# The second block's mixer: attention beside the projection, mLSTM alone behind it

## The reference, cut to what matters

```python
def hybrid_mixer(h, w_in, gate_bias, g_q, g_k, g_mh, w_out):
    proj = h @ w_in          # mq mk mv mo mg aq ak av: 256 256 512 512 16 512 512 512
    gates = ... + gate_bias
    hm = bidirectional_mlstm(mq, mk / 8, mv, gates[0], log_sigmoid(gates[1]), gates[2], log_sigmoid(gates[3]))
    hm = rms_norm(hm, g_mh) * sigmoid(mo)                  # 4 heads, 128 wide
    qa = partial_rope(rms_norm(aq, g_q)) * 64 ** -0.5      # 8 heads, 64 wide
    ka = partial_rope(rms_norm(ak, g_k))
    ha = dilated_attention(qa, ka, av)                     # windows at dilations 1, 4, 16
    return concatenate([hm, ha]) @ w_out
```

## Time and profile before

| what | us |
|---|---|
| median of three runs | 3205.44 |
| the profiled execution | 3206.36 |
| its span, first to last instruction | 3204.4 |
| PE busy in the span | 3104.4 (97%) |
| DVE busy | 1905.7 (59%) |
| ACT busy | 1042.2 (33%) |
| mean granted clock of PE, as a share | 0.985 |
| projection of this mixer (2465.17 to 2631.09) | 165.92 |
| mixed stage (2631.09 to 2783.29) | 152.20 |
| output projection (from 2783.29 to 2835) | 51.71 |

### The profile page before, as it was taken

The page is one execution under the profiler, slowest core; times in us unless marked ns, Lnnn a source line. Parts: engine busy times, 40 slices in busy tenths (PEclk is TensorE's granted clock), DMA queues, the critical chain, the costliest instruction groups (busy, mean ns, idle before and its releaser), DMA issues.

```text
span 3204.4 us, 37150 instructions
## 1 busy us (share of the span) xinstructions
PE 3104.4 (97%) x15012; PEld 2517.3 (79%) x15022; DVE 1905.7 (59%) x2786; ACT 1042.2 (33%) x1525; POOL 9.7 (0%) x23
## 2 busy tenths in 40 slices
PE   8999999998899999999999999999999998899998
PEld 7888888786678888788877888878887765578887
DVE  7876654636665555666657555466665565564434
ACT  4212222435442222422235222332223435442222
POOL 0000000000000000000000000000000000000000
PEclk9999999999999999999999999999999998899999
DMA  6433342210033443256532353235451220133231
GB/s 228 144 119 119 137 146 79 65 52 11 2 125 132 143 173 124 82 178 233 187 117 71 131 186 130 87 115 190 169 215 57 79 66 1 47 121 103 92 99 53
DMA packets 102964, 369.19 MB, mean 115 GB/s; under 512 B 11358, under 2 KB 12638, under 8 KB 102540
## 3 DMA queue, kind: packets, MB, share of 16 engines
q1 hardware_dynamic: 101788, 362.14, 33.2%
q0 software_dynamic: 1008, 4.69, 0.4%
HBM read 364.69 MB, written 2.10 MB: 114 GB/s over the span
## 4 chain that ended last, share of the span: by engine, by line
PE 86%; DVE 8%; ACT 4%; issue 1%; DMA 1%; SPq 0%; POOL 0%; DVEq 0%; ACTq 0%; POOLq 0%
PE ps L193 25%; PE ps L195 24%; PE ps L194 24%; PE ps L197 4%; PE ps L198 2%; DVE SQ L615 1%; DVE HL L604 1%; DVE WL L185 1%; PE ps L2869 1%; DVE XT L1038 1%; DVE RAW L1501 0%; DVE DUMP L306 0%; ACT WH L180 0%; DMA STG<-in_w_modt 0%; PE ps L500 0%
## 5 line engine op out<-in xcount | busy, mean ns | idle before, releaser
L193 PE MATMUL ps<-HH,WH 128*128 128x512 f32 x2400 | 947.2, 395 | 5.4 <-ACT S L915 2.2
L195 PE MATMUL ps<-HH,WL 128*128 128x512 f32 x2400 | 936.4, 390 | 0.0
L194 PE MATMUL ps<-HL,WH 128*128 128x512 f32 x2400 | 936.0, 390 | 0.0
L180 ACT ACTIVATE WH<-RAW 128x1024 fp32r<-128x1024 f32 x456 | 459.0, 1048 | 630.9 <-PE ps L195 361.8
L185 DVE TENSOR_TENSOR WL<-RAW,WH 128x1024 fp32r<-128x1024 f32 x456 | 542.7, 1219 | 75.3 <-ACT WH L180 75.1
L193 PEld LDWEIGHTS ps<-HH,WH 128*128 128x128 f32 x2400 | 450.9, 188 | 111.3 <-issue 10.2
L195 PEld LDWEIGHTS ps<-HH,WL 128*128 128x128 f32 x2400 | 450.9, 188 | 96.8
L194 PEld LDWEIGHTS ps<-HL,WH 128*128 128x128 f32 x2400 | 451.2, 188 | 95.7 <-issue 3.8
L1038 DVE SCALAR_TENSOR_TENSOR XT<-ps,DER,XT 128x512 f32<-128x512 f32 x512 | 346.6, 683 | 246.5 <-PE ps L195 231.7
L193 PE MATMUL ps<-GH,WH 128*128 128x512 f32 x1056 | 414.1, 392 | 4.8 <-DVE GL L946 4.8
L195 PE MATMUL ps<-GH,WL 128*128 128x512 f32 x1056 | 411.1, 389 | 0.0
(11 more groups left out here) (373 smaller groups left out, 2600.0 us busy)
## 6 DMA issues: line engine op xcount, KB each, us to landing
RAW<-in_w_modt SPq DMA_DIRECT2D x200, 512.0 KB, 5.0
RAW<-in_ffn_wi SPq DMA_DIRECT2D x182, 512.0 KB, 4.9
RAW<-in_w_gu SPq DMA_DIRECT2D x90, 512.0 KB, 4.5
RAW<-in_ffn_wo SPq DMA_DIRECT2D x88, 512.0 KB, 4.7
RAW<-in_w_in SPq DMA_DIRECT2D x44, 512.0 KB, 3.6
RAW<-in_w_down SPq DMA_DIRECT2D x44, 512.0 KB, 3.9
RAW<-in_w_out SPq DMA_DIRECT2D x16, 512.0 KB, 4.4
STG<-in_w_modt SPq DMA_DIRECT2D x10, 512.0 KB, 12.9
```

The costliest lines, as they stand in the source:

```text
L180: act.e.activation(u.hi, u.ld.view, ACT.Copy).then_inc(u.hi_done.sem, 1)
L193: pe.e.matmul(out, wh, x[0], start=first, stop=False)
L194: pe.e.matmul(out, wh, x[1], start=False, stop=False)
L195: m = pe.e.matmul(out, wl, x[0], start=False, stop=last)
```

## The change

Attention's steps are put between the halves of the projection's chunks; mLSTM runs behind the projection with nothing beside it.

- `projection` gets `between`, called in the middle of every single chunk and behind its eviction. It draws the next step of `dilated`, which waits with empty steps until its pair's query and key are split.
- The projection has banks 0 and 1, all side work bank 2. `DilTrans` uses banks 6 and 3 from the start. `PP` and `PT` lie in the lent rooms.
- The chunks have another order: DQ, DK, DV and an mLSTM value chunk in turn, then MV3, the four MO, and MQ and MK last.
- `NormedRope` has four parts. Square root and reciprocal become Ln and Exp(-0.5 x) on ACT and three DVE operations (a Newton step); the scaling is a part of its own. One Ln-Exp table is loaded ahead of the projection. The sigmoid of MO moves out of the eviction to `MlSigmoid` behind the projection, and the Ln-Exp table is loaded again behind it.
- `MlExp` is split in `MlWeights` (ACT) and `MlScore` (PE), with weights one round ahead, six places for them instead of four, two score banks (0 and 1) instead of one, and two sets of summing banks by head (2, 3, 4 and 6, 7, 5). The eight broadcasts move from the projection into `mlstm`: two ahead of it and two in each of heads 0 to 2.
- `MixSplit` of attention's four row blocks comes in the rounds of head 1. The last head's quotient, square, root and turn follow the last sum with nothing between.

```diff
 class NormedRope(Step):
...
-            act.e.activation(ti.RS, P.banks[self.b], ACT.Sqrt, scale=1.0 / 64, bias=P.EPSC).then_inc(st["root"].sem, 1)
+            act.e.activation(ti.RS, P.banks[self.b], ACT.Ln, scale=1.0 / 64, bias=P.EPSC).then_inc(self.ln.sem, 1)
+            act.wait_ge(*self.ln)
+            act.e.activation(ti.RS, ti.RS, ACT.Exp, scale=-0.5).then_inc(st["root"].sem, 1)
...
-            dve.e.reciprocal(ti.RS, ti.RS).then_inc(st["inv"].sem, 1)
+            dve.e.scalar_tensor_tensor(v, P.banks[self.b], EPS * 64, r, ALU.add, ALU.mult).then_inc(self.prod.sem, 1)
+            dve.wait_ge(*self.prod)
+            dve.e.scalar_tensor_tensor(v, v, -0.5 / 64, r, ALU.mult, ALU.mult).then_inc(self.half.sem, 1)
+            dve.wait_ge(*self.half)
+            dve.e.scalar_tensor_tensor(r, v, 1.5, r, ALU.add, ALU.mult).then_inc(st["inv"].sem, 1)
...
+class MlSigmoid(Step):
...
+        for h in range(4):
+            act.e.activation(m.O[:, h, :], m.O[:, h, :], ACT.Sigmoid).then_inc(m.opened[h].sem, 1)
...
+    def main(self, h):
+        return 2 if h % 2 == 0 else 6
+
+    def extra(self, h):
+        return 4 if h % 2 == 0 else 5
...
     def projection(self, pr, w, chunks, segs_of, evac, lag, beside=None, depth=1, between=None):
...
+                    if len(chs) == 1 and between:
+                        self.add(ProjMM(pr, [p], range(4)))
+                        between()
+                        self.add(ProjMM(pr, [p], range(4, 8)))
...
                     evac(p)
+                    if len(chs) == 1 and between:
+                        between()
...
-                pr = Proj(self, h, (0, 1, 2, 3), (4, 5, 6, 7))
+                pr = Proj(self, h, (0, 1), (2,))
...
-                order = [DQ, DV, MG, DV + 1, DQ + 1, DV + 2, DV + 3, DQ + 2, MQ, MQ + 1, DQ + 3, MK, MK + 1]
+                order = []
                 for i in range(4):
-                    order += [DK + i, MV + i]
-                order += list(range(MO, MG))
-                self.projection(pr, a["w_in_2"], order, lambda ch: [(0, T)], evac, lag)
...
+                    order += [DQ + i, DK + i, DV + i, MG if i == 0 else MV + i - 1]
+                order += [MV + 3] + list(range(MO, MG)) + [MQ, MK, MQ + 1, MK + 1]
+                self.projection(pr, a["w_in_2"], order, lambda ch: [(0, T)], evac, lag, between=lambda: next(steps, None))
+                for _ in steps:
+                    pass
+                self.add(MlSigmoid(m))
+                self.add(LogExpTable())
...
     def mlstm(self, m, w, mix, w_out):
...
+        for d in range(2):
+            self.add(MlBroadcast(m, 0, d))
+        self.add(MlMask(m, 0))
+        split(0, True)
+        split(0, False)
+        unit[0] = self.add(MlWeights(m, 0, 0))
         self.add(MlFloor(m))
...
+        self.add(MlTurnFloor(m, w.score[15].exp + [w.quot[3].done]))
+        for r in range(16):
+            h, j = r // 4, r % 4
+            self.add(MlScore(m, unit[r]))
+            if h and j == 1:
+                quot[h - 1] = self.add(MlQuot(m, den[h - 1]))
+            if r < 15:
+                unit[r + 1] = self.add(MlWeights(m, (r + 1) // 4, (r + 1) % 4))
+            if h and j == 1:
+                square[h - 1] = self.add(MlSquare(m, quot[h - 1]))
+            if r:
+                last[r - 1] = self.add(MlSum(m, unit[r - 1]))
+            self.add(MlProd(m, unit[r]))
+            if h and j == 0:
+                den[h - 1] = self.add(MlDen(m, last[r - 1]))
+            if h and j == 2:
+                root[h - 1] = self.add(MlRoot(m, square[h - 1]))
+            if h and j == 3:
+                out[h - 1] = self.add(MlOut(m, root[h - 1]))
+            if j == 2 and h < 3:
+                for d in range(2):
+                    self.add(MlBroadcast(m, h + 1, d))
+                self.add(MlMask(m, h + 1))
+            if h == 0 and j in (0, 1):
+                split(1, j == 0)
             if h == 1:
...
+                mixed(4 + j, w.quot[j].done)
+        last[15] = self.add(MlSum(m, unit[15]))
+        den[3] = self.add(MlDen(m, last[15]))
         self.new_ring()
         self.units = self.split([w_out[0]])
...
+        quot[3] = self.add(MlQuot(m, den[3]))
+        for k in range(2):
+            mixed(k, out[k].done)
+        square[3] = self.add(MlSquare(m, quot[3]))
+        root[3] = self.add(MlRoot(m, square[3]))
+        mixed(2, out[2].done)
+        out[3] = self.add(MlOut(m, root[3]))
+        mixed(3, out[3].done)
...
     def dilated(self, w):
...
+                while w.pairs[q][0] not in w.qsplit or w.pairs[q][0] not in w.ksplit:
+                    yield
                 self.add(DilScore(w, q))
-                yield
             if 1 <= q <= last:
                 self.add(DilTrans(w, 2 * q - 2))
-                yield
+            yield
+            if 1 <= q <= last:
...
                 self.add(DilTrans(w, 2 * q - 1))
...
                 self.add(DilPV(w, q - 2))
...
+            if q < last:
+                self.add(DilCount(w, q))
+            yield
```

More of the change, by code:

```diff
@@ L2177, in __init__ @@
             self.rsfree = tiles.rsfree
-            st["sum"] = tiles.sqfree = s["side_mm"].next()
-            st["root"] = pr.sidefree[self.b] = s["nr_act"].next()
-            st["inv"] = s["rope"].next()
+            st["sum"] = s["side_mm"].next()
+            self.ln, st["root"] = s["nr_act"].next(), s["nr_act"].next()
+            self.prod, self.half = s["rope"].next(), s["rope"].next()
+            st["inv"] = tiles.sqfree = s["rope"].next()
+            pr.sidefree[self.b] = self.prod
+        elif part == 2:
             st["scaled"] = tiles.rsfree = s["rope"].next()
@@ L2435, with __init__ @@
 class MlBroadcast(Step):
[L2438 to L2443, removed]
+    def __init__(self, m, h, d):
+        self.m, self.h, self.d, self.b = m, h, d, m.main(h) + d
+        self.split, self.free = m.mgsplit, m.numfree[h % 2]
+        self.spread = m.P.s["ml_mm"].next()
+        self.done = m.P.s["ml_act"].next()
         m.bcast[h, d] = self.done
+        if d == 1:
+            m.numfree[h % 2] = self.done
     def tensor(self, pe):
@@ L2455, in scalar, with __init__ @@
     def scalar(self, act):
+        m, h = self.m, self.h
+        act.wait_ge(*self.spread)
+        act.e.activation(m.MB[self.d * 4 + self.h], m.P.banks[self.b], ACT.Copy).then_inc(self.done.sem, 1)
+class MlSigmoid(Step):
+    def __init__(self, m):
+        self.m = m
+        m.opened = [m.P.s["ml_gate"].next() for _ in range(4)]
+    def scalar(self, act):
         m = self.m
[L2457 to L2460, removed]
+        for h in range(4):
+            act.e.activation(m.O[:, h, :], m.O[:, h, :], ACT.Sigmoid).then_inc(m.opened[h].sem, 1)
 class MlMask(Step):
@@ L2489, in __init__ @@
         for d in range(2):
-            s = m.na % 4
+            s = m.na % 6
             m.na += 1
@@ L2796, in scalar @@
                 act.wait_ge(*w.trans[u - 4].turned)
-            act.e.activation(w.PP[:, u % 4, :], w.P.banks[4 + par], ACT.Exp,
+            else:
+                for t in w.freed:
+                    act.wait_ge(*t)
+            act.e.activation(w.PP[u % 4], w.P.banks[4 + par], ACT.Exp,
                              bias=w.NM[:, s, hs:hs + 1]).then_inc(self.exp[par].sem, 1)
@@ L2845, in scalar @@
         act.wait_ge(*self.free)
-        act.e.activation(w.PT[:, self.u // 2 % 2, self.u % 2, :], w.P.banks[self.b], ACT.Copy).then_inc(self.done.sem, 1)
+        act.e.activation(w.PT[self.u % 4], w.P.banks[self.b], ACT.Copy).then_inc(self.done.sem, 1)
 class DilPV(Step):
@@ L2854, in __init__ @@
         self.j, self.n = w.pairs[q]
-        self.ready = [w.trans[2 * q + par].done for par in range(2)]
+        self.ready = [w.trans[2 * q + par].done for par in range(2)] + [w.turned[self.j]]
         self.done = w.P.s["dil_mm"].next()
@@ L3024, in at, with rooms @@
         return self.nc.alloc_sbuf_tensor_at(self.name(name), shape, dt, offset=address)
+    def rooms(self, places):
+        return [self.over_ring(f"ROOM{i}{part}", [128, 2, T], F32, part + i * 4096)[:, half, :]
+                for i in places for part in (0, NUNIT * 4096) for half in range(2)]
     def name(self, s):
@@ L3306, in follow, with projection @@
         lag.append(g)
-    def projection(self, pr, w, chunks, segs_of, evac, lag, beside=None, depth=1):
+    def projection(self, pr, w, chunks, segs_of, evac, lag, beside=None, depth=1, between=None):
         def job(chs):
@@ new lines, in split @@
+        def split(p, query):
+            x, hi, lo, splits = (m.Q, m.QH, m.QL, m.qsplit) if query else (m.K, m.KH, m.KL, m.ksplit)
+            splits[p] = self.add(HiLo(self, x[:, p, :], hi[:, p, :], lo[:, p, :], []))
+        mixed = lambda k, ready: self.add(MixSplit(self, mix, [k], [ready]))
+        unit, last, den, quot, square, root, out = {}, {}, {}, {}, {}, {}, {}
+        m.numfree[1] = m.turnfree[1] = w.quot[3].done
+        for d in range(2):
+            self.add(MlBroadcast(m, 0, d))
```

200 lines of the change are left out of this document (82 added, 118 removed).

## The result

The changed kernel took 3210.89 us (median of 20 runs, 3206.06 to 3219.80), the kernel before beside it 3205.38 (20 runs, 3200.77 to 3209.18): ratio 1.0020, 95% interval [1.0014, 1.0027]. I had forecast 3202.5, so the sign is wrong and the size is off by 8.4 us. The run that was profiled is the slowest of the 20 (3219.80), so what its trace shows of the clock is a bad case.

The account below looks back on a forecast made before the run. PE, busy 97% of the span, was taken as the bound. Projection +71.8, mixed stage -75.4 and output projection +0.7 gave -2.9 us: 3203.5 against the profiled 3206.36, median 3202.5, range 3188 to 3219.

Parts of the forecast that it names:

- The turns' waits: Projection: in seven chunks the turn behind a rotation waits 0.95 us for DVE's sine product to free the bank.
- the start: Start of mLSTM: a serial ACT chain behind the last projection product, 10.1 us with almost nothing for PE.
- the length of a stall: mLSTM rounds: PE waits 2.15 us for a DVE product in a head's second tile, three times.
- the tail: Behind the last mLSTM sum: the last head's quotient chain leaves PE idle 6.9 us before the last turn.
- the price of attention's PE work: Projection: attention's scores, transpositions, PV steps and spreads add 65.7 us of PE time at full clock.
- one side bank instead of four: Projection: bank waits of 8.3 us, from seven turns, 0.6 for the turn of U and 1 for late counts.
- Rival C: Projection: in-order queues make attention steps wait 2 us at each of eight norm parts, +13, 3219 us; chance 0.09.
- the output projection: Output projection: low clock at its beginning costs 2.5 us, early weight fetch removes the 1.8 us wait; +0.7.
- The clock of the rounds: mLSTM rounds: low clock for 12 us behind the start, +4.8, and 1.5 after each of three stalls, +4.5.
- Rival B: mLSTM rounds: mLSTM alone never earns full clock, stage 90 us, +11.5, 3217; sign granted clock below 0.6; chance 0.18.
- rival A: mLSTM rounds and after: the clock recovers fast and returns 12.2 us, -15, 3190 us; chance 0.24.
- D: End of projection: attention isn't done by the last chunk and runs on alone; three steps to spare; chance 0.02.

Follow-up runs that it names:

- a4: Changed kernel with the gate chunk moved from fourth place to behind the last value chunk: 3207.72 us, ratio 1.0000.
- b2: Changed kernel with two side banks (2 and 3) and one transposing bank (6) in place of one and two: 3202.42 us, ratio 0.9990.
- d4: Changed kernel with the next block's bias sum on DVE in two halves, one output chunk apart: 3206.24 us, ratio 1.0003.
- d1: Changed kernel with late gate chunk, sigmoids and table loads inside the projection, and two extra 128-row products per mLSTM score: 3194.72 us, ratio 0.9970.
- d2: Changed kernel with late gate chunk and sigmoids and table loads inside the projection, without extra products: 3204.15 us, ratio 0.9995.
- a1: Changed kernel with 15 filler products on PE in the pause before the first mLSTM score: 3210.7 us, ratio 1.0008.
- a2: Changed kernel with two extra 128-row products ahead of each mLSTM score: 3205.38 us, ratio 1.0002.
- a3: Changed kernel with both the filled start pause and two extra 128-row products a round: 3208.02 us, ratio 1.0007.

## Why the prediction was wrong

**What held.** The turns' waits (6.1 against 6.7), the hidden work of ACT and DVE in most of the projection, the start (9.7 against 10.1), no pause behind table loads, the length of a stall (1.9 against 2.15), the tail (6.6 against 6.9). a4, in which only the order of the gate chunk differs, has the projection that I forecast to 1 us, but two errors cancel in that: of its 236.92 us PE is busy 225.55, where I had priced 229.4 without waits, and idle 11.4, where I had 8.3. So the price of attention's PE work was right only to about 4 us.

**What failed, in order of size.**

1. In the step "one side bank instead of four", the 0.6 us for the turn of U. It measured 5.64, with low clock behind it: the projection took 243.1 against 237.7, +5.4. I had priced the bank as if the copy came when its producer ended, and didn't write down what stands ahead of it in DVE's queue: two scans, a norm part that they push back, ACT behind that, a weight's split behind ACT. That this queue is the cause, and not the bank's number by itself, is shown by a4 (another place for the gate chunk, and the wait is gone) and b2 (two side banks, and a pause of 5.66 at the same place). Rival C named this mechanism, in the wrong place: not 2 us at each of eight norm parts but 5 us where the gate chunk falls between two of them.
2. In the step "the output projection", the 1.8 us that should go. I took the wait for one on late weights. It was not: ACT had their high half ready at 2815.52, and DVE began the low half only at 2817.48, behind a bias sum, which d4 moves out of the way. The same sum stands in front of the same low half in the trace of the kernel before:

```profile
2802.28 3.61 DVE L752 SCALAR_TENSOR_TENSOR ACC<-RAW,MOD,ACC 128x256 f32<-128x256 f32 x7
...
2802.80 1.04 ACT L180 ACTIVATE WH<-RAW 128x1024 fp32r<-128x1024 f32 x1
...
2805.81 1.22 DVE L185 TENSOR_TENSOR WL<-RAW,WH 128x1024 fp32r<-128x1024 f32 x1
```

3. The clock of the rounds. I took 12 us of low clock behind the start and 1.5 for each stall. It is not a fixed price but varies from run to run: 0.50 through most of the rounds in the profiled run, and 72.6 to 84.8 us in the four traces of the same rounds. Rival B named the place and, for the profiled run (90 forecast, 84.8 measured), about the size; by the sign that I had set for it, a granted clock below 0.6, that run is B's (0.59 over the stretch). That the term was near the middle of the four is luck.

3202.5 + 5.4 + 1.8 = 3209.7, against 3210.9 measured. That the clock's term is right at the median is this sum's word and that of four traces, no more; the median run itself has no trace. From the other side: a4 took 3.2 off the median and d4 4.7. If the two add, which no run shows by itself, they leave 3203.0, near the 3202.5 that I had forecast.

Two slips of the working stand beside this. The range's low end, 3188, is said to be rival A with no stalls in the projection; by the terms above that is 3190 less 8.3, 3182. And the chance of "slower", 0.27, is less than the 0.29 of rivals B, C and D together.

Above the terms stands a wrong reading of the case: I counted the clock as a consequence of pauses alone. d1 and d2 have the same wait ahead of the rounds (3.8 us), and only d1 has the clock back. What PE ran in between decided there. Pauses still count: in a1's trace the clock falls behind a stall. The Trainium skill, "TensorE: Matmul & The Clock Gate", section "A second HAM failure mode: psum-queue depth-cycling", which I had put beside rival B, lays such a swinging clock to small pauses between groups of products; here it stays at 0.50 through 30 us without one pause, so pauses are not all of it. The Trainium skill, "ScalarE: Activation LUTs", section "What ACT_TABLE_LOAD costs", gives a drain of 1380 ns for every switch of the table set; that would be an estimated 2.8 us at the start, which the 0.02 us behind each load above exclude. Why two extra products hold the clock and one seldom does, and why half the rows do so in some runs alone, stays open.

The mistake in 1 and 2 is one: a wait was read by its last releaser and not by the queue ahead of it.

## What to carry to other kernels

When the full-width work beside a stage of small products is taken away, expect that the clock can go with it, and price the stage at both clocks; where it comes out at the low one, a few full-width products more can pay (9.4 us faster for 10 of work here), and where the stage is mixed already they can be pure cost (5.8). When a bank or tile gets one place instead of four, write out the consumer's in-order queue at each place where it is freed, above all where a rare long step (here two scans) falls. And ask of a wait that you mean to remove what stands ahead of it on the releasing engine.

## What the runs showed of the hardware

- TensorE worked without a wait for 30 us (2720 to 2750, changed kernel) in the mLSTM rounds, whose scores have 64 rows and whose sums 129 columns, and was granted 0.50. In a1's fastest run it was granted 1.00 for 17 us of the same rounds (2717 to 2734). With two more products of 128 rows and 512 columns in each round (a2) it had 1.00 from 2730 on.
- The same program on the same chip fell into two heaps: a1 at 3196.7 to 3204.8 with a mean granted clock of 0.984 to 0.988, and at 3209.5 to 3213.1 with 0.981 to 0.983.
- A start bridged with products did not spare the fall: in a3 the clock was 1.00 to 2720 and 0.50 at 2725 to 2735.
- The first operation behind a table load on ScalarE began 0.01 to 0.02 us after the load's end, in three loads of two traces.
